# A two-layer hybrid encoder: branch C's scores over 96 rows at once, keys that start chunk by chunk, one matmul less in the joint, and the final gain as one row

## The reference

```python
h = rms_norm(x, mix_norm_g[l])                       # columns of w_in give q, k, v of A and B, cq, ckv, ckr, gates
oa = diff_attention(aq, ak, av, positions, lam)      # A: 4 heads, two maps each
ob = dilated_attention(bq, bk, bv)                   # B: 8 heads
# C: 8 heads; a query or key of a head is 64 "nope" features and 32 rotary ones
q  = rms_norm(cq, q_norm_g) @ w_uq                   # 8 x (64 + 32)
kv = rms_norm(ckv, kv_norm_g) @ w_ukv                # 8 x (64 + 64)
sc = einsum(q_nope, k_nope) + einsum(rope(q_rope), rope(ckr))   # one rotary key for all 8 heads
oc = softmax(sc * 96 ** -0.5) @ v
x += sum_i(sigmoid(gate_i) * (o_i @ w_branch_i)) @ w_out
x += cross_attention(rms_norm(x), rms_norm(mem), w_xq, w_xkv) @ w_xo     # 4 heads, 256 memory tokens
x += moe(rms_norm(x))                                # 32 experts, two per token, SwiGLU
...
return rms_norm(x, final_norm_g)
```

## Time and profile before

| | |
|---|---|
| median of 3 runs | 1650.2 us (1649.14 to 1651.13) |
| the profiled execution: its time, its span | 1651.03 us, 1649.1 us |
| PE busy, PE loading weights | 1334.7 us (81%), 793.4 us (48%) |
| DVE, ACT, POOL busy | 509.6, 241.1, 33.5 us |
| mean granted TensorE clock | 0.912 of full |
| moved by DMA | 504.41 MB, mean 306 GB/s |

### The profile page before, as it was taken

The page is one execution under the profiler, slowest core; times in us unless marked ns, Lnnn a source line. Parts: engine busy times, 40 slices in busy tenths (PEclk is TensorE's granted clock), DMA queues, the critical chain, the costliest instruction groups (busy, mean ns, idle before and its releaser), DMA issues.

```text
span 1649.1 us, 18201 instructions
## 1 busy us (share of the span) xinstructions
PE 1334.7 (81%) x7594; PEld 793.4 (48%) x7594; DVE 509.6 (31%) x1007; ACT 241.1 (15%) x585; POOL 33.5 (2%) x46
## 2 busy tenths in 40 slices
PE   8999999999666566767699999999995665656655
PEld 7886688755122122233168757886642121312211
DVE  4235464444211212221112462643531211211121
ACT  2214410032010000000021244000410000000001
POOL 2000000001000000000000000000100000000000
PEclk9999999999888778788899999999998887888788
DMA  9933245259999999999995423533899999999996
GB/s 299 327 115 116 77 132 217 102 230 386 413 422 421 421 409 422 421 422 420 419 345 186 121 85 94 198 135 114 328 365 423 421 421 422 420 421 421 421 421 281
DMA packets 141719, 504.41 MB, mean 306 GB/s; under 512 B 9152, under 2 KB 82944, under 8 KB 93504
## 3 DMA queue, kind: packets, MB, share of 16 engines
q1 hardware_dynamic: 137920, 494.41, 76.9%
q0 software_dynamic: 1824, 4.56, 1.0%
q10 hardware_dynamic: 1888, 4.19, 0.7%
HBM read 502.08 MB, written 1.05 MB: 305 GB/s over the span
## 4 chain that ended last, share of the span: by engine, by line
PE 55%; DMA 38%; SPq 2%; DVE 2%; issue 1%; ACT 1%; DVEq 0%; ACTq 0%
DMA ring<-in_w_dram 38%; PE banks L1668 25%; PE banks L1914 6%; PE banks L1974 5%; PE banks L1674 4%; PE banks L2069 3%; SPq L562 2%; PE banks L1816 1%; PE banks L1826 1%; PE banks L1847 1%; PE banks L1868 1%; PE banks L2104 1%; PE banks L2055 1%; PE banks L1726 1%; PE banks L1811 1%
## 5 line engine op out<-in xcount | busy, mean ns | idle before, releaser
L1914 PE MATMUL banks<-ring,v 128*32 128x512 f32 x1920 | 293.0, 751 | 182.5 <-DMA ring<-in_w_dram 175.1
L1668 PE MATMUL banks<-hT,ring 128*128 128x256 f32 x1440 | 317.6, 380 | 0.5 <-ACT kx_wide L821 0.5
L1668 PEld LDWEIGHTS banks<-hT,ring 128*128 128x128 f32 x1440 | 272.0, 190 | 43.1 <-issue 5.0
L1914 PEld LDWEIGHTS banks<-ring,v 128*32 128x32 f32 x1920 | 79.0, 133 | 383.5 <-issue 381.1
L1974 PE MATMUL banks<-ring,probT 128*32 128x512 f32 x960 | 143.9, 723 | 89.8 <-DMA ring<-in_w_dram 84.3
L1974 PEld LDWEIGHTS banks<-ring,probT 128*32 128x32 f32 x960 | 38.2, 129 | 178.7 <-issue 168.2
L1343 DVE COPY q<-banks 128x512 f32<-128x512 f32 x16 | 11.1, 692 | 245.4 <-PE banks L1974 214.5
L1868 PE MATMUL banks<-v,h 128*128 128x128 f32 x512 | 65.8, 289 | 13.5 <-issue 13.2
L1339 DVE TENSOR_TENSOR q<-banks,q 128x512 f32<-128x512 f32 x16 | 11.1, 692 | 212.1 <-PE banks L1914 212.1
L1868 PEld LDWEIGHTS banks<-v,h 128*128 128x128 f32 x512 | 62.4, 202 | 28.0 <-issue 28.0
L1674 PE MATMUL banks<-ring,hT 128*128 128x256 f32 x256 | 57.2, 381 | 0.0
(11 more groups left out here) (312 smaller groups left out, 1286.8 us busy)
## 6 DMA issues: line engine op xcount, KB each, us to landing
ring<-in_w_dram SPq DMA_DIRECT2D x360, 1024.0 KB, 19.2
ring<-in_w_in_dram SPq DMA_DIRECT2D x52, 1024.0 KB, 11.0
ring<-in_w_branch_dram SPq DMA_DIRECT2D x8, 1024.0 KB, 5.1
ring<-in_w_out_dram SPq DMA_DIRECT2D x8, 1024.0 KB, 5.9
ring<-in_w_branch_dram SPq DMA_DIRECT2D x8, 512.0 KB, 3.4
k<-in_w_dram SPq DMA_DIRECT2D x4, 1024.0 KB, 8.5
shared<-in_w_dram SPq DMA_DIRECT2D x4, 1024.0 KB, 12.2
ring<-in_w_dram SPq DMA_DIRECT2D x8, 512.0 KB, 20.7
```

Of the source, the lines that this page charges most:

```text
L1668: last = nc.tensor.matmul(dst, w[:, k, cols], src[:, k, :], start=k == 0, stop=k == kn - 1)
L1914: last = nc.tensor.matmul(bank[2 + m][e * CAP:(e + 1) * CAP, :], xt[:, k, e * CAP:(e + 1) * CAP], ws[e](r), start=k == 0, stop=k == KD - 1)
```

## The change

Four edits.

1. **C's scores over 96 rows.** The nope query and key of every head now lie on partitions 0 to 63 of a tile column of their own, the rotary parts on 64 to 95 below them. A step has two matmuls over 96 rows in place of four. For this ACT takes the even heads (partitions 0 to 63 of PSUM) and DVE the odd ones (64 to 127, written to 0 to 63) of cq0, cq1, ck0 and ck1; before, ACT took cq0, cq1 and ck0 alone and DVE ck1. The last addition of "cr" becomes four, one for each strip. POOL copies the rotated rotary key from head 0 to the seven others (32 partitions x 1792 elements), right behind "kr" in each layer. "cqr" goes through the tile `wide`, and the matrices for the rotation lie in h, so SP issues their load behind slot 0's release instead of before it.
2. **The first memory keys wait by chunk** (`mem_chunk`) instead of for all copies; one of two `stay_warm` goes; the two spreading matmuls come behind both halves and go to bank 5.
3. **The joint** loses its `stay_warm`.
4. **The final gain** is loaded as one row of 4 KB; PE spreads it over the partitions in the last round with two matmuls over one row, ACT copies them to `gain`, and the last combining matmuls, POOL and DVE wait for that.

```diff
-         ("cq0", 15, 0, "act"), ("cqr", 15, 1, "act"), ("cq1", 16, 1, "act"),
-         ("ck0", 17, 0, "act"), ("cr", None, 0, "dve"), ("ck1", 17, 0, "dve"),
+         ("cq0", 15, 0, "act+dve"), ("cqr", 15, 1, "act"), ("cq1", 16, 1, "act+dve"),
+         ("ck0", 17, 0, "act+dve"), ("cr", None, 0, "dve"), ("ck1", 17, 0, "act+dve"),
...
+                        wait_free(sp, l, 0)
                         sp.dma_start(turn_mats, consts[:, C_TURN:]).then_inc(strips_in, 16)
...
+                wait_copied(pool, l, "kr")
+                plain(pool)
+                r = slice(C_NOPE, C_DH)
+                nc.gpsimd.tensor_copy(kc[r, 1:8, :], kc[r, 0:1, :].broadcast_to([C_ROPE, 7, SEQ])).then_inc(setup_pool, 1)
...
-            load_gain(final_norm_g.rearrange("(a n) -> a n", a=1))
-            pool.wait_ge(gain_in, last * 16 + 48)
+            nc.gpsimd.dma_start(gain[0:1, :], final_norm_g.rearrange("(a n) -> a n", a=1)).then_inc(gain_in, 16)
+            pool.wait_ge(row_copied, DEPTH + 1)
...
+                if spread:
+                    act.wait_ge(row_made, DEPTH + 1)
+                    nc.scalar.activation(gain[:, 0:512], bank[0][:, :], ACT.Copy)
+                    nc.scalar.activation(gain[:, 512:1024], bank[1][:, :], ACT.Copy).then_inc(row_copied, 1)
...
                 elif name == "kr":
-                    last = rope(l, 0, kc[:, 4:5, :], b2[:, 0:1, :], b2[:, 1:2, :], 1)
+                    tmp = rope(l, 0, oBC[:, 6:7, :], b2[:, 0:1, :], b2[:, 1:2, :], 1)
+                    last = nc.vector.tensor_tensor(kc[r, 0, :], oBC[r, 6, :], tmp[r, 0, :], ALU.add)
                 elif kind == "ck":
-                    c = 2 * int(i)
-                    last = nc.vector.tensor_copy(kc[:, c:c + 2, :], b2)
+                    c = 4 * int(i) + 1
+                    last = nc.vector.tensor_copy(kc[0:C_NOPE, c:c + 3:2, :], b2[C_NOPE:])
...
                 elif name == "cr":
-                    last = rope(l, 1, q0[:, 4:6, :], q0[:, 4:6, :], b2, 2)
+                    tmp = rope(l, 1, qr, qr, b2, 2)
+                    for strip in range(4):
+                        rows, hd = slice(C_ROPE * strip, C_ROPE * strip + C_ROPE), 2 * (strip % 2) + strip // 2
+                        last = nc.vector.tensor_tensor(q0[r, hd:hd + 5:4, :], qr[rows], tmp[rows], ALU.add)
...
-                    if l > 0 and t == TT - 1:
-                        stay_warm(1, bank[0], C_INV)
...
                 if C0 <= i < X0:
                     for j in range(2):
-                        rows = slice(64 * j, 64 * j + 64)
-                        nc.tensor.matmul(dst[:, j, :], q0[rows, u - 8, qs], kc[rows, u - 8, :], start=True, stop=False)
-                    for j in range(2):
-                        group, at = divmod(u - 8, 2)
-                        rows = slice(64 * j + C_ROPE * at, 64 * j + C_ROPE * at + C_ROPE)
-                        last = nc.tensor.matmul(dst[:, j, :], q0[rows, 4 + group, qs], kc[rows, 4, :], start=False, stop=True)
+                        hd = 2 * (u - 8) + j
+                        last = nc.tensor.matmul(dst[:, j, :], q0[0:C_DH, hd, qs], kc[0:C_DH, hd, :], start=True, stop=True)
...
+                if ends == DEPTH - 1:
+                    pe.wait_ge(gain_in, ends * 16 + 48)
+                    nc.tensor.matmul(bank[0][:, :], ones[0:1, :], gain[0:1, 0:512], start=True, stop=True)
+                    nc.tensor.matmul(bank[1][:, :], ones[0:1, :], gain[0:1, 512:1024], start=True, stop=True)\
+                      .then_inc(row_made, 1)
...
             mem_turn(0, 1)
-            stay_warm(2, bank[2], C_IOTA)
-            mem_turn_copied(0)
+            stay_warm(1, bank[2], C_IOTA)
             mem_keys(0)
```

More of the change, by code:

```diff
@@ L372, in bass_hybrid_encoder @@
         N_MADE = sum(not j[2] for j in JOBS)
-        N_COPIED = {e: sum(j[3] == e for j in JOBS) for e in ("act", "dve")}
+        N_COPIED = {e: sum(e in j[3] for j in JOBS) for e in ("act", "dve")}
         def wait_made(eng, l, name):
@@ L385, in wait_copied @@
             n = JOB_NAMES.index(name)
[L386 to L387 removed]
+            for e in JOBS[n][3].split("+"):
+                eng.wait_ge(copied[e], l * N_COPIED[e] + count_before(lambda j: e in j[3], n))
         def slot_k(j, k, n):
@@ L807, in job @@
                     return
+                elif name == "cqr":
+                    act.wait_ge(ca_rstd, 2 * l + 1)
+                    last = nc.scalar.activation(qr, b2, ACT.Copy, scale=C_DH ** -0.5)
                 elif kind == "cq":
-                    c = 4 if i == "r" else 2 * int(i)
-                    last = nc.scalar.activation(q0[:, c:c + 2, :], b2, ACT.Copy, scale=C_DH ** -0.5)
+                    c = 4 * int(i)
+                    last = nc.scalar.activation(q0[0:C_NOPE, c:c + 4:2, :], b2[0:C_NOPE], ACT.Copy, scale=C_DH ** -0.5)
                 elif kind == "ck":
-                    c = 2 * int(i)
-                    last = nc.scalar.activation(kc[:, c:c + 2, :], b2, ACT.Copy)
+                    c = 4 * int(i)
+                    last = nc.scalar.activation(kc[0:C_NOPE, c:c + 4:2, :], b2[0:C_NOPE], ACT.Copy)
                 elif kind == "cv":
@@ L822, in job, with experts_round @@
                 last.then_inc(copied["act"], 1)
-            def experts_round(S, wait_w1, rd, look, fresh):
+            def experts_round(S, wait_w1, rd, look, fresh, spread=False):
                 def copy_xt(k):
@@ L1705, in job @@
                     for c in range(2):
-                        last = nc.tensor.matmul(b[:, c * SEQ:(c + 1) * SEQ], turn_mats[:, c * P:(c + 1) * P], kr_parts,
+                        last = nc.tensor.matmul(b[:, c * SEQ:(c + 1) * SEQ], turn_mats[:, (c + 1) * P:(c + 2) * P], kr_parts,
                                                 start=True, stop=True)
@@ L1743, in job @@
                     wait_copied(pe, l, "cqr")
-                    last = nc.tensor.matmul(b[:, :], turn_mats[:, 2 * P:3 * P], q0[:, 4:6, :], start=True, stop=True)
+                    last = nc.tensor.matmul(b[:, :], turn_mats[:, 0:P], qr, start=True, stop=True)
                 elif kind == "as":
@@ L1767, in mem_turn_copied, with mem_chunk, mem_row @@
                 pe.wait_ge(memT_dve, l * 2 + 2)
+            def mem_chunk(k):
+                if k % 4 == 0:
+                    pe.wait_ge(memT_act, k // 4 + 1)
+                if k % 4 == 2:
+                    pe.wait_ge(memT_dve, k // 4 + 1)
+            def mem_row(l):
+                pe.wait_ge(mem_diag_made, l * TT + TT)
+                for t in range(TT):
+                    last = nc.tensor.matmul(bank[ROW_BANKS[l]][:, t * P:(t + 1) * P], ones, mem_diag[:, t, :],
+                                            start=True, stop=True)
+                last.then_inc(row_made, 1)
             def mem_keys(l):
@@ L1774, in mem_keys @@
                     pe.wait_ge(mem_w_in, l * 32)
-                features(bank[0][:, 0:SEQ], wxk, slice(0, P), memT, KD)
-                pe.wait_ge(mem_diag_made, l * TT + TT)
-                for t in range(TT):
-                    last = nc.tensor.matmul(bank[1][:, t * P:(t + 1) * P], ones, mem_diag[:, t, :], start=True, stop=True)
-                last.then_inc(mem_row_made, 1)
+                features(bank[0][:, 0:SEQ], wxk, slice(0, P), memT, KD, mem_chunk if l == 0 else None)
+                if l > 0:
+                    mem_row(l)
                 features(bank[0][:, SEQ:2 * SEQ], wxk, slice(P, 2 * P), memT, KD).then_inc(mem_made, 1)
+                if l == 0:
+                    mem_row(l)
             def mem_values(l, tiles=range(TT)):
```

50 lines of the change are left out of this document (30 added, 20 removed).

## The result

The changed kernel takes **1655.3 us** (median of 10, 1652.85 to 1660.55), the kernel before 1650.4 us (10, 1649.14 to 1651.69). The ratio is 1.0032 with a 95% interval of 1.0024 to 1.0040: slower by 4.9 us, more than the 0.2% that was called tellable. I had forecast 1651.0 with a range up to 1654.0 and "the same" as likeliest. The time lies outside the range, on the side to which I had given 0.16.

What follows compares the result with a forecast made beforehand. Saturated DMA (421 GB/s) bounds the expert stages, PE nearly all the rest. Terms -0.7 - 0.1 - 1.4 + 4.2 - 1.2 = +0.8 on a median of 1650.2 gave 1651.0 us, range 1645.8 to 1654.

Steps and rivals of the forecast that it cites:

- what DVE and ACT pay: Attention of each layer: extra DVE and ACT work stops PE about 2.3 us at step 15; nothing later waits.
- POOL's copy: Step 9 of each layer: the copy holds DVE's second c_folded addition and PE's "cs" 2.1 us; +4.2 for two layers.
- pause at step 15: PE waits before the turns, 1.8 us for DVE plus 0.5 for ACT: 2.3 a layer, bounds 1.0 and 2.8.
- start and joint: Keys begin sooner at the start, -0.7, and the first job after the joint starts sooner, -0.1.
- C's scores on PE: Attention: 96-row pairs cost 0.86 us, 0.40 less a step, and tile shapes save 0.4; -3.2 a layer.
- final row: Last expert stage: 512 KB less at 421 GB/s saves 1.25 us; term -1.2, bounds 0 and -1.3.
- distrust: Attention: savings taken whole were trimmed, from -0.9 to -0.7 a layer, so -1.4 for both layers.
- the rival that POOL doesn't get in: Step 9: DVE's second addition goes ahead of POOL's copy, no block; -3.4 alone, 1646.8 us; chance 34%.
- C's net: Attention of each layer: 2.3 stall less 3.2 saved, -0.9, taken as -0.7; both layers -1.4, bounds +2 and -4.
- 1.4 of net delay: Last expert stage: delay from earlier terms, so PE starts about 0.9 us sooner instead of 1.25.
- POOL's slow copy: Step 9 of each layer: the copy costs 2.5 ns an element, 4.5 us; 1655.8 us; chance 8%.
- The third rival: Attention: 96-row score pairs cost 1.01 us and don't pay; 1653.4 us with POOL's block, 1649.2 without; chance 10%.

Runs made afterwards that it cites:

- experiment 3: Changed kernel with three 128x449 products that nobody reads put on PE in front of turn_probs(13); 1653.2 us, ratio 1.0015 to the kernel before.
- experiment 4: Changed kernel with products that nobody reads in both PE pauses, three before turn_probs(13) and two before "cs"; 1650.6 us, ratio 1.0000 to the kernel before.
- both pauses away: Changed kernel with POOL's copy behind both c_folded additions, DVE's four additions split over steps 14 and 16, "ck1" moved later; 1642.8 us.
- the small edits: Kernel before with only the chunk waits at the start, no filling product in the joint, and the final gain as one row; 1648.5 us.
- experiment 1: Changed kernel with one wait more: POOL's copy also waits for DVE's two c_folded additions; 1650.2 us, ratio 0.9997 to the kernel before.
- experiment 12: The both pauses away kernel with DVE's two c_folded additions put in front of the rotation of "kr" in step 8; 1641.3 us.
- experiment 6: Changed kernel with the copy of the 32 turned rows made by ACT instead of POOL, right after "kr"; 1649.85 us.
- experiment 5: Changed kernel with only ACT's half of "ck1" moved behind its probability copy, DVE unchanged; 1653.8 us, ratio 1.0022 to the kernel before.
- experiment 2: Changed kernel with DVE's four 32-row additions moved from step 13 to 14 and ACT's half of "ck1" behind its probability copy; 1651.8 us.

## Why the prediction was wrong

**The step that failed** is in the paragraph on what DVE and ACT pay: "So PE stands still for about 1.8 + 0.5 = 2.3 us at step 15 ... Nothing later waits." Place, releaser and nearly the length were right. What was wrong is to price a pause of PE at its length. The clock fell behind it, and I had thought of the clock only at the joint, where I took the last filling away and where it stayed at 1.0. The sum had no term for it. The term of POOL's copy has the same gap: it lets everything behind "cs" come later "by POOL's whole duration", and no more. Experiments 3 and 4 show it: filling both pauses gives 4.7 us back, filling the pause at step 15 takes its window from 0.50 to 1.00.

**The sum, term by term**, in us for the kernel:

| term | forecast | measured | from |
|---|---|---|---|
| start and joint | -0.8 | -0.2 | start and joint alone |
| C's scores on PE | -6.4 | -5.7 | both pauses away, against the small edits |
| pause at step 15 | +4.6 | +5.3 | idle 2.63, twice |
| POOL's copy | +4.2 | +2.9 | idle 2.21 for 0.74, twice |
| final row | -1.2 | -1.4 | final row alone |
| clock behind the two pauses | none | +4.7 | both pauses filled |
| sum | +0.8 with the 0.4 of distrust | +5.6 (measured 4.9) | |

Without the clock the measured terms come to +0.9. That this is my +0.8 is luck: the scores gave 0.7 us less than forecast, the start and the joint 0.6 less, and the pause cost 0.7 more, while POOL's copy cost 1.3 less, and each measured time has an error of 1 us and more.

- *POOL's copy*: the rival that POOL doesn't get in is wrong. It waits for the first addition (its record starts at 133.88, beside it), then takes its turn, and the second addition waits with its record open, 1.78. The size was off: alone, the copy is 1.67 us (experiments 1 and 12), not the 2.08 of the record beside the additions, which by my reading holds 0.4 of its own wait. That reading is argued. The Trainium skill's figure ("GPSIMD Engine Reference", Elementwise — side-by-side cycle accounting), by which I had estimated 1.5 us, was nearer than my rows' 2.1. On the port the trace agrees with the Trainium skill ("SBUF — State Buffer", SBUF: two separate sides), with 1.78 against 0.42, and experiment 6 agrees with its word that only the port shared by GpSimd and VectorE is contended: ACT's copy beside the same additions leaves them at 0.42.
- *The pause at step 15*: 2.63 us. DVE's four additions put its next instruction 2.81 us after the first of them, instead of 0.60 after the one, so +2.2 and not +1.8: each costs 0.70, not 0.60, within the bound that I had given for instructions that change the partition range. ACT's copy costs the 0.5 forecast (experiment 5).
- *The scores*: at full clock pairs stand 0.86 to 0.87 apart, as the 128-row rows had said, but only where no `products` stand right in front; behind `products`, at four of the eight steps, it is 0.96 to 0.97 (and 0.92 at step 16 in experiment 3). That is 0.1 four times in a layer that I had not counted. Step 20 waits 0.82 for ACT instead of 0.24, as foretold. By whole times the scores save 2.9 us a layer against 3.2 forecast; by the timeline it is 2.7, up to g0 1.1 us and behind it 1.6 (34.1 us from g0 to g3's job against 35.7).
- *Two sums of mine don't follow.* The lower bound of C's net, -4, leaves out my own bound of 0.63 for a pair; with it and a pause of 1.0 it is -7.6. And the "1.4 of net delay" in the paragraph on the final row isn't what the terms before it add up to, which is +2.0. The distinction drawn there, 0.9 instead of 1.25 sooner, doesn't show: PE still waits 1.83 us for the load, and both rows of w2 come 4.4 us later than before.
- *The chances*: I had put 8% on an outcome over 1654, with POOL's slow copy as its only way. The slower side came by a mechanism that had no place among the rivals. That the slow copy's number, 1655.8, lies near the measured 1655.3 is an accident: its copy of 4.5 us took 1.67. The third rival is out as well, since no pair at full clock costs 1.01.

## What to carry to other kernels

A pause of TensorE in a stretch in which it is otherwise busy has two prices: its length, and what follows at half clock. When an edit makes PE wait 2 us or more in a place where it had not (here 2.21 and 2.63), add a term for the clock with a chance, and look at the granted clock behind pauses of that length in the trace of before. Here its mixing stages have no pause of PE over 1 us behind the kernel's first 20 us, and a clock of 1.00, but its expert stages have pauses of up to 7.3 us for weights, and the clock in the earlier trace rows is 0.80. The quickest test is to fill the pause with products that nobody reads: what comes back is the clock's share alone. A saving on one engine that is bought with small instructions on another belongs where that other engine idles: here the same instructions, split by what the next scores really read and put 1 to 3 steps later or, as in experiment 12, into an idle time before, turned +4.9 us into -9.0.

## What was not expected of the hardware

The fall of the clock behind a pause is not certain, even at the same place with the same pause to 0.01 us. In the profiled runs, behind 2.63 us at step 15 it fell in five places of eight (the changed kernel, experiments 1 and 6, and the scores alone, two layers each), and cost 3.1 and 3.0 us in the changed kernel's two and 1.6 in the three others, where the half clock lasted about half as long. Behind 2.21 us at "cs" it fell in six of ten (the changed kernel, experiments 2, 3 and 5, and the scores alone) and cost 1.6 us each time; behind 2.15 us (experiment 5) in neither layer; behind the pauses up to 1.20 us in none. What decides it in one execution isn't settled.

These falls are an obvious reason for the spread of the changed kernel's runs, 7.7 us against 2.6 for those of the kernel before that were taken beside it, and with both pauses filled it is 3.2. But they are not the whole of it, and the rest is open: experiments 1 and 6 both keep the pause of 2.63 us, and their runs spread over 2.7 and 6.7 us. An expert stage varies too: in the kernel with the final row alone, whose layer 0 is that of before, PE needed 2.6 us less from the first matmul of the first expert stage to the joint.
